# Where the half-width expert jobs stand among eight, in a two-layer hybrid mixer and mixture-of-experts kernel

## The reference, cut to what matters

```python
def swiglu(t, w_gate, w_up, w_down):
    return (jax.nn.silu(t @ w_gate) * (t @ w_up)) @ w_down

def moe_ffn(u, router, w_gate, w_up, w_down):
    ...
    logits = (t @ router).astype(jnp.float32)
    top_v, top_e = lax.top_k(logits, TOP_K)          # 2 of 8 experts per token
    top_w = jax.nn.softmax(top_v, axis=-1)
    ...
    def expert_block(args):
        xe, e = args
        return swiglu(xe, w_gate[e], w_up[e], w_down[e])
    ...
    out = jnp.zeros_like(t).at[row_tok].add((yb * row_w[:, None]).astype(t.dtype))
```

## Time and profile before

| | |
|---|---|
| median of 3 runs | 1122.48 us (1122.47 to 1122.56) |
| profiled execution | 1122.31 us |
| its span in the profile | 1120.6 us |
| PE busy | 1081.8 us (97%) |
| PE weight loads busy | 829.8 us (74%) |
| DVE busy | 701.7 us (63%) |
| ACT busy | 634.6 us (57%) |
| POOL busy | 309.2 us (28%) |
| read from HBM | 352.17 MB |
| written to HBM | 9.18 MB |
| share of 16 DMA engines, weight queue (q1) | 79.8% |

### The profile page before, as it was taken

The page is one execution under the profiler, slowest core; times in us unless marked ns, Lnnn a source line. Parts: engine busy times, 40 slices in busy tenths (PEclk is TensorE's granted clock), DMA queues, the critical chain, the costliest instruction groups (busy, mean ns, idle before and its releaser), DMA issues.

```text
span 1120.6 us, 14864 instructions
## 1 busy us (share of the span) xinstructions
PE 1081.8 (97%) x5739; PEld 829.8 (74%) x5739; DVE 701.7 (63%) x758; ACT 634.6 (57%) x756; POOL 309.2 (28%) x338
## 2 busy tenths in 40 slices
PE   7999999999999999999989999999998999999994
PEld 6888888888889877797347897887345898888331
DVE  4876554554568648995017989886016889888112
ACT  7878644443585876774017767775006777776002
POOL 9985200000178765482004003000104001200000
PEclk9999999999999999999999999999998999999998
DMA  9643985526234359999999999999999999999994
GB/s 298 203 157 103 401 319 184 191 100 205 76 111 149 133 225 384 399 413 406 403 414 405 407 413 409 405 411 409 406 411 407 409 410 409 408 407 410 414 403 199
DMA packets 114954, 359.28 MB, mean 321 GB/s; under 512 B 11509, under 2 KB 30127, under 8 KB 104640
## 3 DMA queue, kind: packets, MB, share of 16 engines
q1 hardware_dynamic: 108976, 344.16, 79.8%
q0 software_dynamic: 5728, 13.86, 3.6%
q10 hardware_dynamic: 176, 0.27, 0.1%
HBM read 352.17 MB, written 9.18 MB: 322 GB/s over the span
## 4 chain that ended last, share of the span: by engine, by line
PE 84%; DMA 7%; DVE 3%; ACT 3%; SPq 1%; issue 1%; DVEq 0%; ACTq 0%
PE bank L2836 9%; PE bank L2838 9%; PE bank L2837 9%; PE bank L2894 7%; PE bank L2863 5%; PE bank L2865 5%; PE bank L2864 5%; DMA ring<-in_moe_w_up_dram 4%; PE bank L2306 4%; PE bank L2308 4%; PE bank L2307 4%; DMA ring<-in_moe_w_down_dram 2%; PE bank L2423 2%; PE bank L2425 2%; PE bank L2326 2%; PE bank L2325 2%
## 5 line engine op out<-in xcount | busy, mean ns | idle before, releaser
L2178 DVE TENSOR_TENSOR ring_r<-ring,high 128x2048 fp32r<-128x2048 f32 x112 | 256.0, 2291 | 58.5 <-ACT high L1517 58.0
L1517 ACT ACTIVATE high<-ring 128x2048 fp32r<-128x2048 f32 x112 | 214.6, 1918 | 100.1 <-PE bank L2838 53.9
L2836 PE MATMUL bank<-high,uTh 128*128 128x512 f32 (+2 forms) x500 | 188.0, 376 | 10.5 <-DVE ring_r L2178 10.3
L2838 PE MATMUL bank<-high,uTl 128*128 128x512 f32 (+2 forms) x500 | 185.3, 371 | 0.0
L1082 ACT ACTIVATE high<-ring 128x2048 fp32r<-128x2048 f32 (+1 forms) x65 | 122.7, 1893 | 68.4 <-PE bank L2308 41.9
L868 POOL TENSOR_TENSOR low<-ring,high 128x512 fp32r<-128x512 f32 (+1 forms) x67 | 84.8, 1298 | 196.2 <-ACT high L1082 194.8
L2837 PE MATMUL bank<-ring_r,uTh 128*128 128x512 f32 (+2 forms) x328 | 123.0, 375 | 0.0
L1616 DVE TENSOR_TENSOR low<-ring,high 128x2048 fp32r<-128x2048 f32 (+2 forms) x38 | 85.6, 2258 | 54.7 <-ACT high L1082 52.1
L2836 PEld LDWEIGHTS bank<-high,uTh 128*128 128x128 f32 x500 | 95.0, 190 | 29.8 <-issue 11.7
L2838 PEld LDWEIGHTS bank<-high,uTl 128*128 128x128 f32 x500 | 94.8, 190 | 14.5
L1054 POOL DMA_INDIRECT expert_rows<-yrows,row_idx x5 | 6.8, 1358 | 343.8 <-ACT yrows L1473 343.8
(11 more groups left out here) (501 smaller groups left out, 2296.5 us busy)
## 6 DMA issues: line engine op xcount, KB each, us to landing
ring<-in_moe_w_down_dram SPq DMA_DIRECT2D x61, 1024.0 KB, 19.5
ring<-in_moe_w_up_dram SPq DMA_DIRECT2D x44, 1024.0 KB, 19.8
ring<-in_moe_w_gate_dram SPq DMA_DIRECT2D x44, 1024.0 KB, 18.7
ring<-in_w_in_dram SPq DMA_DIRECT2D x36, 512.0 KB, 6.0
ring<-in_moe_w_up_dram SPq DMA_DIRECT2D x18, 768.0 KB, 18.2
low_raw<-in_moe_w_up_dram SPq DMA_DIRECT2D x12, 1024.0 KB, 19.5
low_raw<-in_moe_w_gate_dram SPq DMA_DIRECT2D x12, 1024.0 KB, 18.7
ring<-in_ffn_w_up_dram SPq DMA_DIRECT2D x22, 512.0 KB, 5.3
```

The lines of the kernel that those rows point to most:

```text
L1517: act.activation(high[:, p % SPLIT, :], moe_slot(j, p), ACT.Copy).then_inc(s["high_ready"], 1)
L2178: dve.tensor_tensor(moe_low(j, p), moe_slot(j, p), high[:, p % SPLIT, :].bitcast(F32), ALU.subtract).then_inc(s["low_ready"], 1)
L2836: pe.matmul(o, xh[:, k, :], bh, start=(k == 0), stop=False)
L2838: last = pe.matmul(o, xl[:, k, :], bh, start=False, stop=(k == KD - 1))
```

## The change

It moves the first and the second half job by one place each: full, full, half, full, full, half, full, half in place of full, half, full, full, half, full, full, half. `JOB_AT` is changed with it so that the half jobs still get ranks 1, 2 and 3, in that order, and the full ones ranks 0, 4, 5, 6, 7. The helpers of `half` take the count of full jobs so far (f) in place of the count of half ones (i).

```diff
-        HALF_JOBS = (1, 4, 7)
-
-        JOB_AT = (0, 1, 4, 5, 2, 6, 7, 3)
+        HALF_JOBS = (2, 5, 7)
+
+        JOB_AT = (0, 4, 1, 5, 6, 2, 7, 3)
...
             full(0, 0, "first")
-            for i in range(2):
-                half(3 * i + 1, i)
-                full(3 * i + 2, 2 * i + 1, "after_half")
-                full(3 * i + 3, 2 * i + 2, "after_full")
+            full(1, 1, "after_full")
+            half(2, 2)
+            full(3, 2, "after_half")
+            full(4, 3, "after_full")
+            half(5, 4)
+            full(6, 4, "after_half")
             eng.wait_ge(s["jobs_ready"], 2)
             n_over = eng.value_load(jobs_i[0:1, 3:4], min_val=0, max_val=OVER)
-            half(E - 1, 2, last=True)
+            half(E - 1, 5, last=True)
...
-            def half(j, i, last=False):
-
-                result_rows(j, 2 * i)
+            def half(j, f, last=False):
+
+                result_rows(j, f - 1)
...
-            def half(j, i, last=False):
+            def half(j, f, last=False):
...
-                    dve.wait_ge(s["silu_ready"], 3 * j + 6 * i + (CHUNKS + 3 + c + 1))
+                    dve.wait_ge(s["silu_ready"], 3 * j + 3 * f + (CHUNKS + c + 1))
...
-                    tokens_low(2 * i + 1)
+                    tokens_low(f)
...
-            def half(j, i, last=False):
+            def half(j, f, last=False):
```

## The result

| | before | after |
|---|---|---|
| median | 1122.47 us (8 runs, 1122.28 to 1122.56) | 1125.76 us (8 runs, 1125.51 to 1126.22) |
| profiled execution | 1122.31 us, span 1120.6 | 1125.68 us, span 1123.9 |

The ratio is 1.0031, with a 95% interval of 1.0021 to 1.0041: slower by 3.3 us. The forecast was 1125.0, with a range from 1122.0 to 1126.8. Both kernels read 352.17 MB and compute the same thing.

What follows compares the result with a forecast made beforehand. The expert stage was taken as DMA-bound, ending when the last weight piece lands. The one nonzero term, +2.5 us from a queue running short late in job 1, added to the 1122.48 us median gave 1125.0 us, range 1122.0 to 1126.8.

Steps and rivals of the forecast that it cites:

- What bounds it: Expert stage, 428 to 1106 us: DMA-bound; the last of 264 weight pieces landing, plus an unchanged tail, sets the time.
- The cover at the end of job 0 and the full job behind it: Job 0's end to job 1's end: 13.4 us to landing, 33 pieces want 10.8, so the stream is 2.5 us late.
- The term of 2.5 us: End of job 1: last piece lands at 625.7 us in place of 623.2, making the DMA stream 2.5 us late.
- The change leaves all of this alone: End of job 0: the 13.4 us from issue to landing, POOL's 1.8 us burst included, stays the same.
- upper bound of 4.0 us: End of job 1: loss if the last piece takes the slower row's 6.5 us, landing at 627.2.
- Rival 2: Late job 1: the shallow queue costs more, with landings of 6.5 us, giving 1126.5 us; chance 11%.
- The Trainium skill's formula: One weight piece: some 2.0 us fixed plus bytes over 436 GB/s, estimated 4.4 us, for a loss of 1.9 us.
- The start of job 1 as a full job: Job 0 to job 1: tokens are ready in time and PE passes without a gap; costed at nothing.
- The other jobs: Jobs 2 to 7: no further shortage, one PE stall instead of two, 6.9 us regained by PE, worth nothing in total.
- Rival 1: Job 1: the shallow queue costs nothing, giving 1122.5 us, or up to 1124 if half true; chance 22%.
- Rival 3: Expert stage: PE sets the end, so removing the stall ahead of job 3 pays, giving 1115.6 us; chance 4%.
- the likeliest case's own range: Whole kernel: the forecast's own mechanism, with 62%, puts the time between 1124.3 and 1125.8 us.

Runs made afterwards that it cites:

- e8: Kernel before, with the third pass (100 of 432 matmuls) left out of job 2's gate and up products: 1122.52 us, ratio 1.000.
- e4: Kernel after, with the third pass (100 of 432 matmuls) left out of job 1's gate and up products: 1122.25 us, ratio 0.9999 to before.
- e1: Kernel before with only the first half job moved, from place 1 to 2: 1125.79 us, ratio 1.003.
- e9: Kernel after, with POOL's scatter and gather at the start of job 2 put off until 14 of its pieces are used: 1126.12 us, ratio 1.0034 to before.
- e12: Kernel after run once more, unchanged, on another chip: 1126.07 us, ratio 1.0033 to before.
- e2: Kernel before with only the second half job moved, from place 4 to 5: 1122.32 us, ratio 1.000.
- e5: Kernel after with one place of the weight ring taken away, 15 in place of 16: 1128.73 us, ratio 1.0056 to before.
- e7: Kernel before with four places of the weight ring taken away, 12 in place of 16: 1132.05 us, ratio 1.0091.

## Why the prediction was right, and where it was off

*What bounds it.* Right. e8 shows that PE's work isn't in the total, and e4 that the new loss is one of issue rate.

*The cover at the end of job 0 and the full job behind it.* Right in mechanism, place and sign: 5.0 us to landing from about 600 us on, 366 GB/s over the last 20 us (374 and 359) where 364 was forecast, and by e1 the whole loss in this step. (364 is a piece each 2.88 us; the "2.55 / 2.88 of it" beside it gives 361.) The rate column sagged earlier than forecast, to 374 from 590 us on, and still read 377 from 620 to 630. The term of 2.5 us was mis-sized: it measured **3.4** (1109.7 against 1106.3 for the last landing). The step that failed is "it lands no earlier than 625.7 with 5.0 us. [...] From the next piece on [...] the delay neither grows nor shrinks": the last load at the floor took 5.7 us, behind one of 5.9, and the next one came 2.9 us later instead of 2.55, as e9 shows. "The change leaves all of this alone" was not quite so either: POOL's burst behind job 0 came 2.5 us later (scatter at 529.6 for 527.1 us), and the load issued at job 0's end took 12.4 and 13.0 us in e9 and e12 for 13.4. That starts the shortage earlier but doesn't set the loss, since the last piece of job 1 is issued at 620.4 us either way. My upper bound of 4.0 us, from the one slower load of the earlier trace rows, held it. Rival 2 names that direction, but its mark, landings of over 6 us all along the floor, isn't there.

*The Trainium skill's formula* ("DMA: Bandwidth & Descriptors", "Anatomy of one DMA"), fitted for the GpSimd path, gives an estimate of 4.4 us for a piece and would have given a loss of 1.9 us. The trace doesn't agree for this path: the floor under SP's loads is 4.9 to 5.0 us.

*The start of job 1 as a full job.* Right: PE is busy 94.81 of job 1's 94.90 us.

*The other jobs.* No further shortage, as forecast: 408 or 409 GB/s in jobs 3 to 6, and e2 loses nothing. One stall instead of two, worth nothing: right. But job 7 starts 3.8 us earlier (its first matmul at 1036.8 us against 1040.6), not 6. The first half job, with the stall behind it gone, gave 4.6 us (59.3 against 63.9), the four full jobs behind job 0 gave 1.8 between them (382.1 us against 383.9), and job 5 took 2.5 back: it needs 64.9 us to its last matmul where the second half job before needed 62.4. The last waits of that job are for landings in both traces, so its end moves with the stream, and the stream is 3.4 us late; I had put the delay on the last landing alone. In the last job it waits for them again.

*Rival 1*, the shallow queue that costs nothing, had the second largest chance. It fell with e4 and e5. e2 shows why it was a fair one: near the floor, at 5.9 to 8.8 us, a queue is indeed free. Only at the floor does it cost. *Rival 3* fell with e8 and e2.

*The chances.* 0.55 for slower by over 0.2% was fair: at +0.29% the result lies within 0.1% of that border. The single value of 1125.0 was 0.8 us low by the mis-sized term, and the result lies just inside the likeliest case's own range, whose end was 1125.8.

## What to carry to other kernels

In this stream, which is bound by its transfers, the order of quick and slow consumers cost nothing until the time from issue to landing fell to that of a lone transfer. So in such a stream read it at the end of each slow stretch, subtract the floor, and compare what is left with the number of pieces times the difference of the two rates (here 8.4 us of cover against 10.8 us). Read the rate for a warning and the landing times for the loss, add what a stay at the floor costs beyond the count (about 1 us here), and put the quick jobs where the cover is least, not where the slow engine's stalls are.

## What the runs showed of the hardware

- A sagging rate need not be lost time: 390 GB/s for 27 us in e2, with landings at 5.9 to 8.8 us, cost nothing that could be measured, and the pieces still landed 2.54 us apart. The share of the DMA engines read 1.01 in the same rows, and 0.99 to 1.01 even at the floor.
- The floor for one weight piece on SP's queue is sharp: six loads in a row at 4.9 or 5.0 us in the kernel after and in e9, and 5.0 to 5.4 us in e12, the same kernel on another chip.
- A load at the floor took 5.9 or 6.0 us where a transfer of the queue q8 (instruction) of 1.1 us on one engine fell beside it (e5, e7, e9, e12). With a deep queue it left no mark. No run isolates this.
- Behind the floor the next piece came 2.9 us later, not 2.55 (e9). The stay at the floor cost 0.9 us beyond the count of pieces in the kernel after, and in e7 1.4 at the first place and 1.9 at the other two together; that amount was seen, not isolated.
